# x's token-major form in a Mamba-2 layer: from PE transposes to DVE block transposes and a DRAM round trip

## The reference, cut to what matters

```
zxbcdt = h @ w_in                                  # z (2048), x (2048), B and C (4 x 128 each), dt (32)
xbc = silu(causal_dwconv(xbc, conv_w, conv_b))     # 4 taps along the tokens
dt  = softplus(dt_raw + dt_bias);  xdt = x * dt
decay = exp(seg)                                   # seg[l, s] = a_cs[l] - a_cs[s], causal
y_diag = einsum("bcgls,bcgrls,bcsgrp->bclgrp", C B^T, decay, xdt)
states = einsum("bclgn,bcgrl,bclgrp->bcgrpn", B, decay_to_end, xdt)
y_off  = einsum("bclgn,bcgrpn,bcgrl->bclgrp", C, previous state, exp(a_cs))
y = (y_diag + y_off + D * x) * silu(z);  grouped RMSNorm;  y @ w_out
```

## Time and profile before

| | |
|---|---|
| median of 3 runs | 1107.36 us (1107.17 to 1107.75) |
| profiled execution | 1107.1 us, span of its instructions 1105.3 us |
| PE | 1093.8 us busy, 99% of the span |
| DVE | 570.3 us, 52% |
| ACT | 468.5 us, 42% |
| POOL | 593.3 us, 54% |
| DMA, queue of SP | 115.83 MB, 31.3% of 16 engines |
| mean granted clock of PE | 0.998 |

### The profile page before, as it was taken

One profiled execution on the slowest core, in us unless ns is written; L12 is line 12 of the kernel. 1 busy time (PEld: TensorE's weight loads), 2 busy tenths in 40 slices (PEclk: granted clock), 3 DMA queues, 4 the chain that ended last, 5 costly groups with the idle time before them and its releaser, 6 DMA issues.

```text
span 1105.3 us, 15325 instructions
## 1 busy us (share of the span) xinstructions
PE 1093.8 (99%) x5156; PEld 898.0 (81%) x5156; DVE 570.3 (52%) x640; ACT 468.5 (42%) x804; POOL 593.3 (54%) x448
## 2 busy tenths in 40 slices
PE   9999999999999999999999999999999999999997
PEld 7788888888888788788788878888888888888886
DVE  5665421455423284666777856666664224554123
ACT  7433222233333338558595774343332222333332
POOL 3766544444565635337364474656665444445653
PEclk9999999999999999999999999999999999999999
DMA  7223232222222225333324333222222222323232
GB/s 286 83 99 103 89 101 96 95 95 95 95 95 95 95 77 156 126 105 124 130 92 141 122 107 106 96 95 95 95 95 95 95 95 95 98 99 101 93 104 77
DMA packets 40085, 117.05 MB, mean 106 GB/s; under 512 B 4080, under 2 KB 11888, under 8 KB 40048
## 3 DMA queue, kind: packets, MB, share of 16 engines
q1 hardware_dynamic: 39616, 115.83, 31.3%
q10 hardware_dynamic: 432, 0.73, 0.2%
HBM read 114.32 MB, written 2.23 MB: 105 GB/s over the span
## 4 chain that ended last, share of the span: by engine, by line
PE 97%; DMA 1%; DVE 1%; POOL 1%; issue 0%; ACT 0%; ACTq 0%; DVEq 0%; POOLq 0%
PE bank L832 30%; PE bank L833 30%; PE bank L834 30%; PE bank L1023 1%; PE bank L1032 1%; PE bank L1040 1%; DMA params<-params 1%; PE bank L982 1%; PE bank L873 1%; POOL residual L739 0%; PE bank L1000 0%; PE bank L853 0%; PE bank L961 0%; PE bank L991 0%; DVE residual L1223 0%
## 5 line engine op out<-in xcount | busy, mean ns | idle before, releaser
L712 POOL TENSOR_TENSOR w_lo<-w_raw,w_hi 128x512 fp32r<-128x512 f32 x372 | 499.4, 1348 | 464.2 <-ACT w_hi L437 451.8
L437 ACT ACTIVATE w_hi<-w_raw 128x512 fp32r<-128x512 f32 x372 | 230.6, 626 | 403.9 <-PE bank L834 397.7
L832 PE MATMUL bank<-x_hi,w_hi 128*128 128x512 f32 x848 | 336.1, 396 | 1.7 <-DVE x_lo L1133 1.5
L834 PE MATMUL bank<-x_hi,w_lo 128*128 128x512 f32 x848 | 330.6, 390 | 0.0
L833 PE MATMUL bank<-x_lo,w_hi 128*128 128x512 f32 x848 | 330.5, 390 | 0.0
L832 PE MATMUL bank<-act_hi,w_hi 128*128 128x512 f32 (+1 forms) x656 | 254.5, 388 | 0.0
L834 PE MATMUL bank<-act_hi,w_lo 128*128 128x512 f32 (+1 forms) x656 | 252.2, 384 | 0.0
L833 PE MATMUL bank<-act_lo,w_hi 128*128 128x512 f32 (+1 forms) x656 | 252.1, 384 | 0.0
L832 PEld LDWEIGHTS bank<-x_hi,w_hi 128*128 128x128 f32 x848 | 159.3, 188 | 39.2 <-issue 4.9
L833 PEld LDWEIGHTS bank<-x_lo,w_hi 128*128 128x128 f32 x848 | 159.4, 188 | 34.1 <-issue 2.1
L834 PEld LDWEIGHTS bank<-x_hi,w_lo 128*128 128x128 f32 x848 | 159.3, 188 | 33.3
(11 more groups left out here) (154 smaller groups left out, 683.4 us busy)
## 6 DMA issues: line engine op xcount, KB each, us to landing
w_raw<-weights SPq DMA_DIRECT2D x186, 512.0 KB, 3.3
m<-acs_scratch SPq DMA_DIRECT2D x16, 512.0 KB, 4.4
decay_in<-eacs_scratch SPq DMA_DIRECT2D x24, 128.0 KB, 3.7
x_token<-x_tok SPq DMA_DIRECT2D x4, 512.0 KB, 6.3
residual<-xt SPq DMA_DIRECT2D x8, 256.0 KB, 9.9
out_first<-scaled_residual SPq DMA_DIRECT2D x4, 256.0 KB, 2.4
out_second<-output_rows SPq DMA_DIRECT2D x4, 256.0 KB, 2.7
pooling_matrices<-pooling ACTq DMA_DIRECT2D x2, 288.0 KB, 5.1
```

What stands on the lines that cost most here:

```text
L437: act.activation(whi[:, c % 2, part], raw[:, c % 2, part], ACT.Copy).then_inc(hi_ready, 1)
L712: pool.tensor_tensor(wlo[:, c % 2, part], raw[:, c % 2, part], whi_f[:, c % 2, part], ALU.subtract).then_inc(lo_ready, 1)
L832: pe.matmul(out, wh, xh, start=start, stop=False)
L834: return pe.matmul(out, wl, xh, start=False, stop=stop)
```

## The change

x is brought to token-major form without PE. DVE transposes each x tile in 32x32 blocks into y_accumulated's tiles of the group (`transpose_blocks`), SP writes the blocks to a DRAM scratch in four DMAs of 32 partitions, in pieces of 512 bytes (`write_blocks`), and reads them back token-major into the same tiles in one DMA (`read_tokens`). DVE's `token_x` multiplies them by dt from there, in two halves a chunk. As y_accumulated holds them until then, `skip` moves behind all four x_dt, to t = 3.

To have x early, the convolutions of a group run in the order x0 to x3, B, C. x's silu has its own place: for group 0 behind ACT's first tap of unit 4, for the others at t = 8 of the group before. The block transposes stand behind unit 5's taps and at the head of t = 9. In slot 8 DVE does chunk 3's m before `after_chunk` of chunk 2. PE loses its 16 transposes of x a group; `chunk` takes over the waits on banks.

```diff
--- before.py
+++ after.py
@@ -54,7 +54,8 @@
 TIMES_CB_IN = {4: 1, 6: 2, 8: 3}
-T_TOKEN, T_LATE_TOKEN = 1, 2
+T_TOKEN = 1
+Q = 32
 T_STAT, T_NORM = 4, 7
@@ -182,13 +183,13 @@
         acs_dram = nc.dram_tensor("acs_scratch", [GROUPS, CHUNKS, HPG, P], F32).ap()
+        x_dram = nc.dram_tensor("x_scratch", [GROUPS, CHUNKS * (P // Q), Q, P // Q, GT * Q], F32).ap()
         eacs_dram = nc.dram_tensor("eacs_scratch", [GROUPS, CHUNKS, HPG, P], F32).ap()
...
         b_misc, b_yd, b_yo, b_st, b_stat = bank[3], bank[4], bank[5], bank[6], bank[7]
-        XT_BANK = (b_yd, b_yo, b_st, b_misc)
@@ -249,7 +250,9 @@
         cb_mm = sem("cb_product")
-        x_mm = sem("x_transposed")
+        xt_blocks = sem("x_blocks_transposed")
+        xt_written = sem("x_blocks_written")
+        xt_landed = sem("x_token_major_landed")
         xdt_ready = sem("x_dt_ready")
@@ -314,10 +317,14 @@
+        def x_blocks(g):
+
+            return yx[:, GT * g:GT * g + GT, :].rearrange("p i t -> p (i t)").rearrange("p (n f) -> p n f", f=GT * Q)
+
         def conv_out(n):
...
             g, q = divmod(n, CONVS)
-            return bf[:, :] if q == 0 else cf[:, g % 2, :] if q == 1 else xact[:, q - 2, :]
+            return xact[:, q, :] if q < GT else bf[:, :] if q == GT else cf[:, g % 2, :]
@@ -347,6 +354,21 @@
                                  heads[:, half, :, :].to_broadcast([64, GT, P])).then_inc(e_landed[c % 2], 16)
+
+            def write_blocks(g):
+
+                sp.wait_ge(xt_blocks, g + 1)
+                blocks = x_blocks(g)
+                for a in range(P // Q):
+                    sp.dma_start(x_dram[g, :, :, a, :].rearrange("n q f -> q n f"),
+                                 blocks[Q * a:Q * a + Q, :, :]).then_inc(xt_written, 16)
+
+            def read_tokens(g):
+
+                sp.wait_ge(xt_written, 16 * (P // Q) * (g + 1))
+                sp.dma_start(yx[:, GT * g:GT * g + GT, :],
+                             x_dram[g].rearrange("(c b) q a f -> (b q) c (a f)", c=CHUNKS)
+                             ).then_inc(xt_landed, 16)
@@ -376,6 +398,7 @@
             load_ahead(5)
+            write_blocks(0)
             sp.wait_ge(scratch, 2 * GROUPS * 16)
@@ -385,6 +408,10 @@
                     load_ahead(slot_of(g, t))
+                    if t == PER_GROUP - 1 and g + 1 < GROUPS:
+                        write_blocks(g + 1)
+                    if t == 0:
+                        read_tokens(g)
                     c = chunk_after.get(t)
@@ -565,6 +592,10 @@
+            def silu_x(g):
+                act.wait_ge(acc_drained, A_SSM + conv_slot(CONVS * g + GT - 1) + 1)
+                act.activation(xact[:, :, :], xact[:, :, :], ACT.Silu).then_inc(x_act, 1)
+
             for u in range(CONVS):
@@ -583,20 +614,18 @@
                     act.activation(ones_r[:, :], ones, ACT.Copy).then_inc(ones_ready, 1)
+                if u == 4:
+                    silu_x(0)
...
-                for q in range(2):
+                for q in range(GT, CONVS):
                     act.wait_ge(acc_drained, A_SSM + conv_slot(CONVS * g + q) + 1)
...
-            def silu_x(g):
-                act.wait_ge(acc_drained, A_SSM + conv_slot(CONVS * g + CONVS - 1) + 1)
-                act.activation(xact[:, :, :], xact[:, :, :], ACT.Silu).then_inc(x_act, 1)
-
             def skip(g):
-                act.wait_ge(x_act, g + 1)
+                act.wait_ge(xdt_ready, 4 * g + 4)
                 for i in range(GT):
@@ -647,7 +676,6 @@
                         silu_b_c(g)
-                        silu_x(g)
                         if g:
@@ -659,9 +687,11 @@
                     ahead(u, 1)
+                    if not ends and t == 8:
+                        silu_x(g + 1)
                     if not ends and t >= GT:
                         first_tap(CONVS * (g + 1) + t - GT)
-                    if t == 0:
+                    if t == 3:
                         skip(g)
@@ -976,17 +1006,11 @@
-            def token_x(g, c):
-
-                for i in range(GT):
-                    last = pe.transpose(XT_BANK[c][:, P * i:P * i + P], xact[:, i, P * c:P * c + P], ident)
-                last.then_inc(x_mm, 1)
-
             def token_major(g):
...
                 if g:
-                    pe.wait_ge(xdt_ready, 4 * g)
+                    pe.wait_ge(bt_ready, g)
                 for c in range(CHUNKS):
@@ -1000,24 +1024,17 @@
                 last.then_inc(cb_mm, 1)
-                pe.wait_ge(x_act, g + 1)
-                if g == 0:
+
+            def c_chunk(g, c):
+                return cf[:, g % 2, P * c:P * c + P]
+
+            def chunk(g, c):
+
+                pe.wait_ge(m_ready, 4 * g + c + 1)
+                pe.wait_ge(xdt_ready, 4 * g + c + 1)
+                if g == 0 and c == 0:
                     pe.wait_ge(acsf_ready, 1)
                 else:
-                    pe.wait_ge(y_add, 4 * g)
-                    pe.wait_ge(y_dec, 3 * g)
-                    pe.wait_ge(state_ready, 3 * g)
-                for c in range(CHUNKS - 1):
-                    token_x(g, c)
-
-            def c_chunk(g, c):
-                return cf[:, g % 2, P * c:P * c + P]
-
-            def chunk(g, c):
-
-                pe.wait_ge(m_ready, 4 * g + c + 1)
-                pe.wait_ge(xdt_ready, 4 * g + c + 1)
-                if c:
                     pe.wait_ge(y_add, 4 * g + c)
@@ -1026,7 +1043,7 @@
                     pe.wait_ge(state_ready, 3 * g + c)
-                    if c > 1:
+                    if g or c > 1:
                         pe.wait_ge(y_dec, 3 * g + c - 1)
@@ -1035,8 +1052,8 @@
                     pe.wait_ge(bt_ready, g + 1)
-                    if c == 0:
-                        pe.wait_ge(xdt_ready, 4 * g + 3)
+                    if g and c == 0:
+                        pe.wait_ge(state_ready, 3 * g)
                     pe.matmul(b_st[:, :], bt[:, c, :], dec[:, c % 2, :], start=True, stop=True).then_inc(st_ready, 1)
@@ -1052,9 +1069,6 @@
                         token_major(g)
-                    if t == T_LATE_TOKEN:
-                        pe.wait_ge(bt_ready, g + 1)
-                        token_x(g, CHUNKS - 1)
                     if t == T_STAT and g:
@@ -1253,6 +1267,15 @@
                                              ).then_inc(acc_drained if k == 0 else conv_step, 1)
+
+            def transpose_blocks(g):
+
+                dve.wait_ge(x_act, g + 1)
+                blocks = x_blocks(g)
+                for i in range(GT):
+                    last = dve.transpose(blocks[:, :, Q * i:Q * i + Q],
+                                         xact[:, i, :].rearrange("p (n j) -> p n j", j=Q))
+                last.then_inc(xt_blocks, 1)
@@ -1296,6 +1319,8 @@
                 conv_taps(u)
+                if u == 5:
+                    transpose_blocks(0)
@@ -1318,10 +1343,18 @@
-                dve.wait_ge(x_mm, 4 * g + c + 1)
-                dve.tensor_tensor(by_head(xdt[:, c, :]), by_head(XT_BANK[c][:, :]),
-                                  of_group(dt_t[:, :, :].rearrange("p c h -> p (c h)"), c, g, HD), ALU.mult
-                                  ).then_inc(xdt_ready, 1)
+                dve.wait_ge(xt_landed, 16 * (g + 1))
+                if g and c == 0:
+                    dve.wait_ge(yd_ready, 4 * g)
+                    dve.wait_ge(dec_ready, 3 * g)
+                out = xdt[:, c, :].rearrange("p (i h a j) -> p h i a j", h=2, a=2, j=Q)
+                landed = yx[:, GT * g + c, :].rearrange("p (h a i j) -> p h i a j", h=2, a=2, j=Q)
+                dt = dt_t[:, c, HPG * g:HPG * g + HPG].rearrange("p (i h) -> p h i", h=2)
+                for half in range(2):
+                    last = dve.tensor_tensor(out[:, half], landed[:, half],
+                                             dt[:, half].unsqueeze(2).unsqueeze(3).to_broadcast([P, GT, 2, Q]),
+                                             ALU.mult)
+                last.then_inc(xdt_ready, 1)
@@ -1355,6 +1388,8 @@
                 dve.wait_ge(e_landed[c % 2], 32 * (2 * g + (c == 3) + 1) if c % 2 else 32 * (g + 1))
+                if g or c > 1:
+                    dve.wait_ge(y_done, 3 * g + c - 1)
                 dve.tensor_tensor(tiles(ytmp[:, :]), tiles(b_yo[:, :]), e2[:, c % 2, :, :], ALU.mult
@@ -1423,6 +1458,8 @@
                         after_chunk(g - 1, CHUNKS - 1)
+                    if t == PER_GROUP - 1 and not ends:
+                        transpose_blocks(g + 1)
                     if t == 1 and g:
@@ -1430,13 +1467,13 @@
                         token_x(g, 2)
-                    if t == 3:
-                        token_x(g, 3)
                     if t == T_STAT + 1 and g:
                         invert_group(g - 1)
+                    if t == 8:
+                        decay_times_cb(g, TIMES_CB_IN[t])
                     if t - 1 in CHUNK_AFTER and (ends or t < PER_GROUP):
                         after_chunk(g, CHUNK_AFTER[t - 1])
-                    if t in TIMES_CB_IN:
```

(6 more changed lines are left out.)

4 lines of the change are left out of this document (2 added, 2 removed).

## The result

The changed kernel takes **1126.64 us** (median of 5 runs, 1124.75 to 1128.46) against 1107.36 beside it: a ratio of 1.0172 [1.0161, 1.0184], slower. The forecast of 1113.4 had the sign and the place, and under a third of the size; the time is also above its range, 1105 to 1124. The profiled execution has a span of 1125.1 us against 1105.3, so 19.8 us are to be explained.

A forecast was written before the change was run, and what follows sets the result against it. PE was taken as the bound, busy 1093.8 of 1105.3 us. From 1107.1: - 6.7 transposes + 9.8 group 0 stall + 1.9 clock + 1.0 later groups = 1113.1, with 0.3 for the median 1113.4 us; range 1105 to 1124.

The forecast's parts named there:

- Removed: PE's queue in the SSM stage: transposes and restarts go, 1.68 us a group, 6.7 us in four groups.
- Blocks and landing in group 0: Group 0's round trip: blocks ready at 427.5 us, 4.2 MB to pass, read landed at 445.4.
- the issue of the read: SP's queue in group 0: the read issued at 434.7 us, behind writes, m, decay_in and weights.
- The products after the landing: DVE before chunk 0: six half products 2.2 us, gate_in 0.6, m 1.9, together 4.7 us.
- the wait forecast, 9.8: PE's stall before group 0's chunk 0: m ready at 450.1, wanted at 440.3; bounds 4.5 and 19 us.
- Groups 1 to 3: PE's waits before chunk 0 in the later groups: 1.0 us for the three together, bounds 0 and 12.
- the spare of 2.6: Group 1: m ready at 505.6 us, chunk wanted at 508.2, so 2.6 us to spare.
- near nothing: Groups 2 and 3: fuller DVE, about 5 us less slack at the landing, leaving almost no spare.
- Rival C: DVE becomes the bound: group 0's stall 17 us, each later group adds 4; 1131.6 us, chance 0.12.
- The clock: PE's granted clock falls to 0.5 after group 0's stall: 1.9 us lost, bounds 0 and 4.
- The reordering: Moving skip to t = 3 costs nothing; the last chunk's m first gains nothing on PE.

The follow-up runs named there:

- e9: e7 with GpSimd's sum over the groups adding only 8 of its 512 columns, so the output is not the reference's: 1101.9 us.
- e4: The changed kernel with x transposed on PE again in all four groups, the rest of the change kept: 1107.18 us.
- e8: e7 with groups 2 and 3 transposed on PE as well, so only group 1 makes the round trip: 1105.98 us.
- e2: The changed kernel with chunk 0's m ahead of the other x_dt products on DVE, GpSimd's chunk 1 decayed product behind its splits: 1119.56 us.
- e7: The changed kernel with group 0 transposed on PE, e2's order in groups 1 to 3, ACT's squares behind the decays, the read ahead of the weights: 1110.92 us.
- e12: e7 with each chunk's x_dt product in groups 1 to 3 as one DVE instruction instead of two halves: 1109.96 us.
- e1: The changed kernel with throwaway 512-column products on PE before chunk 0 in groups 0, 2 and 3, about as long as its waits: 1121.25 us.
- e10: e7 with GpSimd's sum moved behind its decayed product of chunk 1, nothing left out: 1113.16 us.
- e11: e10 with the statistics of the group before one slot later: 1114.47 us.

## Why the prediction was right in sign and far too low

**Removed: right.** The transposes are gone, and 6.7 us fits: with three groups' worth (5.0) taken away and next to nothing waiting, e9 is 5.4 us below before (its profiled execution, the slowest of four, 4.5); with all put back, e4 stands on before.

**Blocks and landing in group 0: right; the issue of the read: 3.1 us off.** Silu slipped C's first tap to 421.72 (said: 421.9), four transposes took 2.48 us (2.5), the blocks were ready at 427.2 (427.5), and the read landed at 445.84 (445.4). It was issued at 437.8, though, not at 434.7: SP's issues of the two m loads (2.43 us against 0.81) and of the weights (1.96 against some 0.35) took longer than before. The landing came out because the sum took it from the bytes (4.2 MB) and not from the issue. The 1.2 to 1.4 us in which nothing moves behind an issue were misread, too: in the trace of before it is 0.9 to 1.0 us for the weights (issue at 496.44, first bytes at 497.3) and less for the writes here; the sum used 1.1, so little hung on it. A transpose took 672 ns at the median: the nearest row, the old 128x512 product of the earlier trace rows, was the right one. The Trainium skill's "VectorE: DVE Perf Modes", "The three transpose paths", led to an estimate of 5.0 us for the four, and the trace does not agree with that scaling: 2.48. The rule of the same page of the Trainium skill, "Rules for kernel authors", which sends a 128x128 transpose to TensorE, held in groups 0, 2 and 3, but not by the price of the transpose; in group 1 alone the round trip gained 1.3 us (e8).

**The products after the landing: this term was mis-sized, and it is where the missing time in all four groups begins.** "Six half products of 256 elements at 0.43 less the overlap, 0.36 each, are 2.2 us" rests on a row of two operands, 426 ns, whose surroundings I did not look at. Measured are 3.8, 4.0, 5.6 and 5.0 us. I had the slow rate in hand, 1.81 to 0.69 for two operands in SBUF, and used it for the bound alone. The old x_dt products read a bank (0.67 to 0.68 us each in all four groups); the new ones have both operands in SBUF, and GpSimd's list in that slot is full: from group 1 on the sum over the groups, and in every group the decayed products and the splits. e2, e7 and e9 show the two prices for the same instructions: 0.38 apiece with GpSimd still, 1.3 beside it; m 1.22 or 2.30. e12 shows the form of the cost: up to 1.1 us for each instruction, whatever its size. So it hits small ones hardest, and the change cuts each product in two. In group 0 the 1.6 us by which the products ran over are about the whole difference between the wait forecast, 9.8, and the 11.4 measured.

The Trainium skill has this rule, and I did not weigh it: "SBUF — State Buffer", section "Who interferes with whom", says that a DVE instruction with two inputs in SBUF contends with a GpSimd instruction that reads SBUF, that the shared ports are an exclusive lock, and that the order of issue decides which of the two blocks. The traces agree: an excess of at most 1.12 us against GpSimd operations of 1.04 to 1.3, none on products with one operand in a bank (L1435 stays at 0.66 to 0.69), and GpSimd delayed where DVE came first (e7's 2.03 us, e12's 3.78).

**Groups 1 to 3: 1.0 forecast, 7.9 measured, the largest miss in the waits.** The step that failed is again the products at 2.2 us, and in group 1 also the read at 5.7 us. In group 1 the read was issued where I had it relative to PE, but took 7.2 us instead of 5.7 and the products 1.8 more, and the spare of 2.6 became a wait of 0.64. In group 2 DVE was through with its earlier work at 583.4 and the read landed at 583.92: the slack "near nothing" was right. Landing to m ready then took 7.8 us instead of 4.7, and PE, which wanted m at 588.0, waited 3.8; without the 3.1 us it would have waited 0.7. Rival C named this mechanism with 4 us for each later group. I gave it 0.12 because "a transpose reads one operand", which is true of the transpose and says nothing about the product.

**The clock: 1.9 forecast, 7.2 left over, 6.6 to 6.9 of it shown by e1.** Two things failed. I let the clock fall once, in the longest wait; it fell at the waits of 3.8 and 3.5 us as well. And I priced it with the sixteen opening matmuls, while in group 0 PE worked for about 5.9 us at the lower level, which costs half of that, 3 us. "TensorE: Matmul & The Clock Gate" of the Trainium skill, Part 1, has the rule that an idle array loses the upper level and has to earn it back; the windows above agree, and the price has to be counted for each wait.

**The reordering: right.** e4 shows that silu ahead, skip at t = 3 and the last chunk's m first cost nothing and gain nothing.

The sum with the measured terms, 1107.1 - 6.7 + 11.4 + 7.9 + 7.2 = 1126.9 us, is the profiled execution's span of 1125.1 and 1.8 around it. It must be, since the 7.2 is what was left over; the check on that term is e1. Of the 13.8 us that the forecast's 1113.1 lacks, 6.9 lie in the waits of groups 1 to 3, 5.3 in the clock and 1.6 in the wait of group 0.

What stays open: the 0.3 to 0.6 us that e1 did not give back, and whether another layout of DVE's and GpSimd's lists would bring a complete kernel to the 1101.9 us of e9; e10, e11 and e12 are three that do not.
